# The last two experts of the first mixture-of-experts stage: added to all tokens by one-hot products in place of two indirect stores, and the residual sums loaded earlier

## The chip, the cores and the metric

The kernel runs on one core of one Trainium2 chip. The metric is the device time of one execution in microseconds (us), given as the median of several runs. One execution was profiled; the core's engines are TensorE (PE in the rows, its weight loads PEld), VectorE (DVE), ScalarE (ACT), GpSimd (POOL) and SyncE (SP, which here only starts transfers).

## The reference, cut to what matters

Two decoder layers over 512 tokens of 1024 numbers. Each layer is a mixer and then a hierarchical mixture of 16 experts (of 4 groups one is taken, and of its 4 experts two), both added to the residual x:

```
for layer in range(2):
    h = rms_norm(x, mix_norm)
    x = x + mixer(h)                       # layer 0: state space + gated recurrence; layer 1: sliding-window attention
    h = rms_norm(x, moe_norm[layer])
    # per token: one group, two of its experts, weights "combine"
    hid = silu(h @ w_gate[e]) * (h @ w_up[e]) * combine[:, e]
    x = x + sum over e of hid @ w_down[e]
```

The place of this case is the seam between the first layer's experts and the second layer's attention: `rms_norm(x, ...)` of the second layer needs every expert's contribution to x.

## The kernel before, in words

Tokens stand in four tiles of 128 (TT = 4). A layer's experts (function `experts`, one for each engine) run one after the other, e = 0 to 15. For each one GpSimd fetches up to 128 token rows from a table in memory by an indirect transfer (L479, rows by the list `rows32`), TensorE turns them (`row_turns`, L1906), and multiplies them by gate and up weights (`gate_up`, L1924); ScalarE and VectorE make the gated hidden values; TensorE turns these (`hid_turns`, L1932) and multiplies them by the down weights (`down`, L1948). Every product is made of three f32r products (high and low parts of both operands), so weights and rows are split by ScalarE (high part) and VectorE (low part, by a subtraction).

`down(e)` leaves 128 rows of 1024 results in banks 4 and 5 of PSUM. ScalarE copies them to `yrow[e % 2]` (`result_rows`, L763), and GpSimd adds them to the token rows in memory by an indirect accumulating transfer (`store`, L483). In the first layer that memory is `sums`, into which the residual x was written before the experts began. The store of expert e signals `stored[e % 2]`. GpSimd starts store e once store e - 4 has landed, and ScalarE refills a buffer once its last store has landed.

After the experts each engine passes `experts_over`: it loads a flag into a register (L333) and branches over a body that is only for experts with more than 128 rows (L334). On these inputs the body is not run. Then ScalarE waits for both `stored` semaphores, all 16 stores of the layer (`load_sums`, L800), and loads `sums` into x in four transfers (L802). `norm(2)` on ScalarE takes each tile as it lands: sum of squares (L584), square root (L586), VectorE's reciprocal (L915), the scaled copy `xs` (L596). TensorE turns `xs` (`turn_tile`, L1590), VectorE multiplies by the gain into `hT` (L905), and TensorE makes queries, keys and values (`project`, L2013). `turn_tile(1, 0)` and `project(0, ...)` come first in TensorE's order; the other three tiles are turned behind them.

Weights come through a ring of six slots of 1 MB, refilled by SyncE (L372) as slots are given back. The order on each engine is the order of the code; nothing is reordered.

Of the kernel before, what the change touches and what calls it, by code (L numbers as in the profile page):

```python
# [17 lines left out]
NG, EPG = 4, 4  # L18
# [62 lines left out]
def trunk(nc, x_d, stream_d, cread_d, const_d, param_d, gains_d, out_d):  # L81
# [3 lines left out]
    with ctx:  # L85
        def sb(name, n, dt=f32):
            return ctx.enter_context(nc.sbuf_tensor(name, [P, n], dt))
# [32 lines left out]
            odd.enter_context(nc.sbuf_tensor("odd1", [P, 21504 - 11904 - SLOT], f32))  # L120
            odd_hi = odd.enter_context(nc.sbuf_tensor("odd_hi", [P, SLOT], f32r))[:, :]
        left_hi, left_lo = cut(sb("left_hi", KD * SEQ, f32r), 0, KD, 512), cut(sb("left_lo", KD * SEQ, f32r), 0, KD, 512)
        sb("kept0", 2048)
        w_hi1, w_lo1 = sb("w_hi1", SLOT, f32r), sb("w_lo1", SLOT, f32r)
        sb("kept1", 13312 - 2048 - 2 * SLOT)
        w_hi2, w_lo2 = sb("w_hi2", SLOT, f32r), sb("w_lo2", SLOT, f32r)
# [13 lines left out]
        def out_lo(layer, s):  # L140
            return odd_lo if layer and s == 1 else w_lo[(s + 1 - layer) % 2]

        def expert_pair(layer, m):
            return (2, 1 - layer, layer)[m % 3]

        left_flat = left_hi.rearrange("p k n -> p (k n)")
        row_hi, row_lo = [[cut(left_flat, 1024 * (2 * i + j), KD, 128) for j in range(2)] for i in range(2)]
        low_flat = left_lo.rearrange("p k n -> p (k n)")
        hid_hi, hid_lo = [cut(low_flat, 2560 + 256 * i, 2, 128) for i in range(2)]
        PS = ctx.enter_context(nc.psum_tensor("PS", [P, 8, 512], f32))  # L150

# [90 lines left out]
        w_pair, w_rows, over_weights = sm(2, TT), sm(NE), sm(OVER_TILES)  # L242
        ranks, beyond, flag_f = sm(2 * TT), sm(2 * TT), sm(1)
        group_exp, gap4, gap, gate_sum, pair_sum = sm(TT, 4), sm(TT, 4), sm(TT), sm(TT), sm(TT)
        picked_rank, absent = sm(2 * TT, 16), sm(NE)
        assert at[0] <= 1000, at[0]

        at[0] = S5_END
# [51 lines left out]
        sums_in, weighed, weights_psum = sem("sums_in"), sem("weighed"), sem("weights_psum")  # L300
        rows_made, late_in, first_row_in = sem("rows_made"), sem("late_in"), sem("first_row_in")
        stored = [sem(f"stored{i}") for i in range(2)]

        over = [{n: sem(f"over_{n}{layer}") for n in ("hot", "list_psum", "listed", "weights", "row", "xT_psum", "xT", "gate_up",
                                                      "silu", "hid", "hidT_psum", "hidT", "y_psum", "yrow", "stored")}
# [20 lines left out]
        def used(layer, m):  # L326

            return (NE * EXP_SLOTS + 1) * layer + 1 + m + 1

        def if_over(engine, layer, body):  # L330

# [44 lines left out]
        def _(pool):  # L376
# [109 lines left out]
            def experts(layer):  # L486
                send_rows(layer)
                pool.wait_ge(first_row_in, 16 * (layer + 1))
                pool.wait_ge(rows_in, 16 * (TT - 1) * (layer + 1))
                pool.wait_ge(route_done, layer + 1)  # L490

                def fetch_rows(e):
                    if e >= 2:

                        pool.wait_ge(xT_psum, layer * NE + e - 1)
                    fetch(e % 2, rows32[:, e:e + 1]).then_inc(got_row[e % 2], 16)


                for e in range(4):
                    fetch_rows(e)  # L500
                for e in range(NE):
                    if e + 4 < NE:
                        fetch_rows(e + 4)

                    if e == 0:
                        pool.wait_ge(sums_in, 16 * TT * (layer + 1))
                    if e >= NG:
                        pool.wait_ge(stored[e % 2], 16 * (NE // 2 * layer + (e - NG) // 2 + 1))
                    pool.wait_ge(yrow_done, layer * NE + e + 1)
                    store(layer, e % 2, rows32[:, e:e + 1]).then_inc(stored[e % 2], 16)  # L510

            def experts_over(layer):
                def body(s):
                    for j in range(2):
                        pool.wait_ge(stored[j], 16 * (NE // 2) * (layer + 1))
                    pool.wait_ge(s["listed"], OVER // P)

                    def expert(e, gate_up_at, down_at):

                        pool.dma_start(over_w[:, 0:2 * SLOT].rearrange("p (s n) -> p s n", n=SLOT),  # L520
                                       stream_d[bass.ds(gate_up_at, 2), :, :].rearrange("s p n -> p s n")).then_inc(s["weights"], 16)
                        pool.dma_start(over_w[:, 2 * SLOT:3 * SLOT],
                                       stream_d[bass.ds(down_at, 1), :, :].rearrange("a p n -> (a p) n")).then_inc(s["weights"], 16)
                        for r in range(OVER // P):
                            q = e * (OVER // P) + r
                            nc.gpsimd.tensor_copy(row_now[:, :], over32[:, bass.ds(q, 1)])
                            pool.drain()
# [12 lines left out]
                if_over(pool, layer, body)  # L540
# [2 lines left out]
            experts_over(0)  # L543

            pool.wait_ge(x_in[TT - 1], 48)
            nc.gpsimd.memset(kT1[:, 0:128], 0.0)
            nc.gpsimd.memset(vpad, 0.0).then_inc(at_zero, 1)

# [8 lines left out]
                nc.gpsimd.tensor_tensor(pr, pr, inverse, ALU.mult).then_inc(p_norm, 1)  # L557
            experts(1)
            for j in range(2):
                pool.wait_ge(stored[j], 16 * NE)  # L560
            experts_over(1)


# [1 line left out]
        def _(act):  # L565
# [22 lines left out]
            def norm(occ):  # L588

                for tt in range(TT + 1):  # L590
                    if tt < TT:
                        act.wait_ge(x_in[tt], 48 if occ else 16)
                        deviation(occ, tt, xs[:, tt, :])
                    if tt >= 1:
                        act.wait_ge(rstd_done, TT * occ + tt)
                        act.activation(xs[:, tt - 1, :], x[:, tt - 1, :], ACT.Copy, scale=rstd[:, tt - 1:tt]).then_inc(xs_done, 1)  # L596
# [142 lines left out]
            def experts(layer):  # L739
# [19 lines left out]
                def result_rows(e):  # L759
                    act.wait_ge(w_used, used(layer, down_slot(e)))  # L760
                    if layer or e >= 2:
                        act.wait_ge(stored[e % 2], (base // 2 + e // 2) * 16)
                    act.activation(yrow[e % 2], PS[:, 4:6, :].rearrange("p a b -> p (a b)"), ACT.Copy).then_inc(yrow_done, 1)  # L763

                expert_hi(layer, 2)
                row_his(0, base)
# [1 line left out]
                silu(0)  # L768
                expert_hi(layer, 3)
                for e in range(NE):  # L770
                    if e:
                        result_rows(e - 1)
                    hidden_his(base + e)
                    if e + 1 < NE:
                        expert_hi(layer, down_slot(e))
                    if e + 2 < NE:
                        expert_hi(layer, gate_slot(e + 2))
                        row_his(e % 2, base + e + 2)
                    if e + 2 == NE:
# [17 lines left out]
            def load_sums():  # L797

                for j in range(2):
                    act.wait_ge(stored[j], 16 * (NE // 2))  # L800
                for tt in range(TT):
                    act.dma_start(x[:, tt, :], sums_d[P * tt:P * (tt + 1), :]).then_inc(x_in[tt], 16)  # L802

# [97 lines left out]
        def _(dve):  # L901
# [506 lines left out]
            def experts_over(layer):  # L1408
# [19 lines left out]
                        V.tensor_copy(hidT, PS[:, 3, 0:256].rearrange("p (a b) -> p a b", b=128)).then_inc(s["hidT"], 1)  # L1428
                if_over(dve, layer, body)

            residual(0)
            route(0)
            experts(0)
            experts_over(0)
            for tt in range(TT + 1):
                if tt < TT:
                    inverse(2, tt)
                if tt >= 1:
                    scaled(1, tt - 1)
# [124 lines left out]
        def _(pe):  # L1564
# [333 lines left out]
            def experts(layer):  # L1898
# [36 lines left out]
                def down(e):  # L1935
                    m = down_slot(e)
                    n = base + e
                    pe.wait_ge(hidT_done, n + 1)
                    if layer or e >= 1:
                        pe.wait_ge(yrow_done, n)  # L1940
                    pe.wait_ge(w_lo_done, held(layer, m))
                    pair = expert_pair(layer, m)
                    for half in range(2):
                        for k in range(2):
                            at = k * D + half * 512
                            w = [v[pair][:, at:at + 512] for v in (w_hi, w_lo)]
                            for t, (a, b) in enumerate(((hid_hi[:, k, :], w[0]), (hid_hi[:, k, :], w[1]), (hid_lo[:, k, :], w[0]))):
                                ins = mm(PS[:, 4 + half, :], a, b, start=k == 0 and t == 0, stop=k == 1 and t == 2)  # L1948
                    ins.then_inc(w_used, 1)

                row_turns(0, base, (base // 2 + 1) * 16)
# [45 lines left out]
            experts(0)  # L1997
            experts_over(0)

            turn_tile(1, 0)  # L2000
            def project(tt, part, ks):

# [251 lines left out]
```

## Time and profile before

| | before |
|---|---|
| median of 3 runs | 914.8 us (914.49 to 915.94) |
| the profiled execution | 914.96 us |
| its span, first to last instruction | 913.3 us |
| TensorE busy (matmuls) | 792.9 us, 87% |
| VectorE busy | 584.5 us, 64% |
| ScalarE busy | 476.4 us, 52% |
| GpSimd busy | 172.1 us, 19% |

Busy shares are averages over stages. The first layer's experts run from about 300 to 475 us, attention from about 490 to 670, the second layer's routing and experts after that. Places are given in us from the span's start. A line L763 is line 763 of the kernel before. Small lines are often helpers: L905 is every VectorE operation on two tensors, L908 one with a scalar, L911 one with both, told apart by the tiles they name.

### The profile page before, as it was taken

To read this page: it belongs to the slowest core of one execution; us is meant where nothing else is said; L and a number is where in the kernel's file an instruction comes from. 1 tells how busy PE (TensorE), PEld (TensorE's weight loads), DVE (VectorE), ACT (ScalarE), POOL (GpSimd) and SP (SyncE) were. 2 spreads that over 40 slices of the span, in tenths; PEclk is the share of its full clock that TensorE was granted. 3 is DMA by queue.
4 is the path that set the end of the run, shared out by engine and by line. 5 is a ranking of instruction groups with operands and counts; after the bars stand their busy time and mean duration, and the time that the engine had idled before them with its cause. 6 is when DMAs were issued, how large, how long until landed. Compare 5 with 4: busy or idle time off the path is not lost. (4 is left out here: it accounts for less than half of the span.)

```text
span 913.3 us, 10825 instructions
## 1 busy us (share of the span) xinstructions
PE 792.9 (87%) x4112; PEld 552.4 (60%) x4112; DVE 584.5 (64%) x795; ACT 476.4 (52%) x647; POOL 172.1 (19%) x172
## 2 busy tenths in 40 slices
PE   4999999999897499999972898999899569999983
PEld 3464554554686378877751544545578558887762
DVE  3799756668236488988750356455624649997972
ACT  6051204626224188878744136675733338886872
POOL 4300004100002124333220001030100303332321
PEclk9999999999898599999995999999999679999997
DMA  9222020215425779999983000025043749999962
GB/s 374 98 93 93 2 93 7 86 46 198 195 93 207 287 244 338 329 329 302 328 282 117 1 1 0 1 73 205 1 165 115 312 172 324 338 350 310 318 210 36
DMA packets 31737, 161.50 MB, mean 177 GB/s; under 512 B 7744, under 2 KB 7872, under 8 KB 16320
## 3 DMA queue, kind: packets, MB, share of 16 engines
q1 hardware_dynamic: 17856, 127.93, 37.3%
q0 software_dynamic: 11520, 25.20, 9.9%
q10 hardware_dynamic: 2304, 7.60, 2.2%
q8 instruction: 36, 0.59, 0.3%
q14 instruction: 21, 0.17, 0.1%
HBM read 152.31 MB, written 25.17 MB: 194 GB/s over the span
## 5 line engine op out<-in xcount | busy, mean ns | idle before, releaser
L905 DVE TENSOR_TENSOR w_lo<-ring,w_hi 128x2048 fp32r<-128x2048 f32 x92 | 209.4, 2288 | 53.5 <-ACT w_hi L612 27.8
L1924 PE MATMUL PS<-w_hi,left_hi 128*128 128x512 f32 x512 | 177.1, 408 | 9.2 <-DVE left_hi L905 8.7
L612 ACT ACTIVATE w_hi<-ring 128x2048 fp32r<-128x2048 f32 x86 | 164.1, 1915 | 26.6 <-DMA ring<-stream 25.1
L1924 PEld LDWEIGHTS PS<-w_hi,left_hi 128*128 128x128 f32 x512 | 98.2, 192 | 32.0 <-DVE left_hi L905 12.8
L1924 PE MATMUL PS<-w_lo,left_hi 128*128 128x512 f32 x256 | 101.6, 397 | 0.0
L1948 PE MATMUL PS<-w_hi,left_lo 128*128 128x512 f32 x256 | 85.0, 393 | 5.9 <-DVE left_lo L905 3.3
L2013 PE MATMUL PS<-ring,hT 128*128 128x512 f32 (+1 forms) x192 | 73.6, 536 | 2.7 <-DVE arena L1449 1.9
L479 POOL DMA_INDIRECT arena<-rows x32 | 48.7, 1522 | 82.1 <-PE PS L1906 65.9
L1948 PEld LDWEIGHTS PS<-w_hi,left_lo 128*128 128x128 f32 x256 | 48.1, 188 | 17.9 <-issue 4.2
L1640 PE MATMUL PS<-ring,hT 128*128 128x512 f32 x128 | 57.6, 600 | 0.4 <-ACT arena L668 0.4
L2013 PEld LDWEIGHTS PS<-ring,hT 128*128 128x128 f32 x192 | 36.3, 194 | 35.9 <-issue 33.3
L1640 PE MATMUL PS<-hT,ring 128*128 128x512 f32 x128 | 56.2, 596 | 0.0
L1924 PEld LDWEIGHTS PS<-w_lo,left_hi 128*128 128x128 f32 x256 | 49.2, 192 | 8.3
L905 DVE TENSOR_TENSOR left_hi<-PS,left_hi 128x1024 fp32r<-128x1024 f32 x32 | 39.0, 1219 | 23.4 <-ACT left_hi L748 23.4
L748 ACT ACTIVATE left_hi<-PS 128x1024 fp32r<-128x1024 f32 x32 | 32.4, 1011 | 33.8 <-PE PS L1906 33.8
L1948 PE MATMUL PS<-w_lo,left_lo 128*128 128x512 f32 x128 | 49.9, 390 | 0.0
L668 ACT ACTIVATE arena<-PS 128x512 f32<-128x512 f32 x16 | 9.5, 593 | 76.5 <-PE PS L1640 76.5
L1822 PE MATMUL PS<-w_hi,left_hi 128*128 128x512 f32 x112 | 46.2, 412 | 3.2 <-DVE left_lo L905 2.4
L483 POOL DMA_INDIRECT sums<-hT,rows x16 | 28.3, 1766 | 91.8 <-ACT hT L763 86.7
L483 POOL DMA_INDIRECT out<-hT,rows x16 | 28.2, 1763 | 91.3 <-ACT hT L763 91.3
L1822 PE MATMUL PS<-w_hi,left_lo 128*128 128x512 f32 x112 | 44.7, 399 | 0.0
L763 ACT ACTIVATE hT<-PS 128x1024 f32<-128x1024 f32 x32 | 32.7, 1023 | 22.8 <-PE PS L1948 22.8
(260 smaller groups left out, 1355.0 us busy)
## 6 DMA issues: line engine op xcount, KB each, us to landing
ring<-stream SPq DMA_DIRECT2D x110, 1024.0 KB, 14.1
arena<-stream SPq DMA_DIRECT2D x6, 1024.0 KB
rows<-arena POOLq DMA_DIRECT2D x8, 512.0 KB, 3.1
x<-stream SPq DMA_DIRECT2D x4, 1024.0 KB
x<-x_in SPq DMA_DIRECT2D x4, 512.0 KB, 5.2
x<-x_in ACTq DMA_DIRECT2D x4, 512.0 KB, 6.0
sums<-x POOLq DMA_DIRECT2D x4, 512.0 KB, 4.5
x<-sums ACTq DMA_DIRECT2D x4, 512.0 KB, 5.2
```

The costliest lines, as they stand in the source:

```text
L479: return pool.indirect_dma_start(xrow[j], None, rows_d[:, :], bass.IndirectOffsetOnAxis(index, 0), bounds_check=SEQ - 1, oob_is_err=False)
L483: return pool.indirect_dma_start((sums_d, out_d)[layer][:, :], bass.IndirectOffsetOnAxis(index, 0), yrow[j], None, bounds_check=SEQ - 1, o ...
L612: act.activation(w_hi[pair], held_slot(layer, m), ACT.Copy).then_inc(w_hi_done, 1)
L668: act.activation(dst, PS[:, 7 if i >= 12 else 6 + i % 2, :], ACT.Silu if i // 4 in (1, 3) else ACT.Copy)\
L748: act.activation(row_hi[j], PS[:, 0:2, :].rearrange("p a (b c) -> p (a b) c", c=128), ACT.Copy)\
L763: act.activation(yrow[e % 2], PS[:, 4:6, :].rearrange("p a b -> p (a b)"), ACT.Copy).then_inc(yrow_done, 1)
L905: return V.tensor_tensor(out, a, b, op)
L1640: ins = mm(PS[:, 7 if i >= 12 else 6 + i % 2, :], lhsT[:, m], rhs, start=k == 0, stop=k == KD - 1)
L1822: ins = mm(mixed(layer, s // 2, tt), a, b, start=k == 0 and n == 0, stop=k == KD - 1 and n == 2)
L1924: ins = mm(PS[:, 2, :], a, b, start=k == 0 and t == 0, stop=k == KD - 1 and t == 2)
L1948: ins = mm(PS[:, 4 + half, :], a, b, start=k == 0 and t == 0, stop=k == 1 and t == 2)
L2013: ins = mm(PS[:, 2 + part, 0:n], hT[:, k, tt * 128:tt * 128 + 128], w, start=k == 0, stop=k == KD - 1)
```

## The change

- `experts` on GpSimd no longer stores e = 14 and 15 of the first layer, so each `stored` semaphore counts seven stores there (`stores(1)` = 112).
- ScalarE copies these two experts' results to `last_hi[0]` and `last_hi[1]` (f32r), and VectorE's `split_last` makes their low parts `last_lo` from PSUM. It also builds two one-hot matrices of 128 x 512 from the row lists: a 1 where a row's token is that column's.
- Expert 15's `down` of the first layer goes to banks 6 and 7 and no longer waits for ScalarE's copy of expert 14. In both layers ScalarE takes `hidden_his(15)` before `result_rows(14)`.
- Behind `experts_over(0)` TensorE multiplies, for each token tile, the one-hot matrices by the high and low parts of both experts (`spread`: 32 products of 512 columns). VectorE adds each PSUM tile to x once it is loaded (`add_last`), and the norm waits for that (`summed_in`) in place of the load; for tiles 2 and 3 also for the last product.
- `load_sums` waits for the fourteen stores. GpSimd's two memsets for attention wait for the last product too.

```diff
+        def y_at(layer, e):
+            return 6 if layer == 0 and e == NE - 1 else 4
+        last_hi = [left_flat[:, 2048:3072], low_flat[:, 1024:2048]]
+        last_lo = [left_flat[:, 3072:4096], low_flat[:, 3072:4096]]
+        def stores(layer):
+            return 16 * (NE // 2 - 1) * layer
# GpSimd, experts
+                    if e >= NE - 2 and layer == 0:
+                        continue
                     pool.wait_ge(yrow_done, layer * NE + e + 1)
                     store(layer, e % 2, rows32[:, e:e + 1]).then_inc(stored[e % 2], 16)
# GpSimd, before attention
             pool.wait_ge(x_in[TT - 1], 48)
+            pool.wait_ge(last_psum, TT)
# ScalarE, norm
-                        act.wait_ge(x_in[tt], 48 if occ else 16)
+                        if occ:
+                            act.wait_ge(summed_in, tt + 1)
+                            if tt >= 2:
+                                act.wait_ge(last_psum, TT)
+                        else:
+                            act.wait_ge(x_in[tt], 16)
# ScalarE, experts
                 for e in range(NE):
+                    if e == NE - 1:
+                        hidden_his(base + e)
                     if e:
                         result_rows(e - 1)
-                    hidden_his(base + e)
+                    if e < NE - 1:
+                        hidden_his(base + e)
# ScalarE, load_sums
-                    act.wait_ge(stored[j], 16 * (NE // 2))
+                    act.wait_ge(stored[j], stores(1))
# VectorE
+            def split_last(j):
+                if j == 0:
+                    V.tensor_copy(last_row, rows32[:, NE - 2:NE])
+                    dve.drain()
+                    dve.wait_ge(xT_psum, NE)
+                    for n in range(2):
+                        ts(one_hot[:, n, :], con("time"), last_row[:, n:n + 1], ALU.is_equal)
+                dve.wait_ge(yrow_done, NE - 1 + j)
+                tt_(last_lo[j], PS[:, 4 + 2 * j:6 + 2 * j, :]..., last_hi[j], ALU.subtract).then_inc(last_split, 1)
+            def add_last(tt):
+                dve.wait_ge(x_in[tt], 48)
+                dve.wait_ge(last_psum, tt + 1)
+                at = (4, 0, 2, 6)[tt]
+                tt_(x[:, tt, :], x[:, tt, :], PS[:, at:at + 2, :]..., ALU.add).then_inc(summed_in, 1)
             experts(0)
+            split_last(0)
+            split_last(1)
             experts_over(0)
+            add_last(0)
+            add_last(1)
             for tt in range(TT + 1):
+                if tt + 2 < TT:
+                    add_last(tt + 2)
                 if tt < TT:
                     inverse(2, tt)
# TensorE, down
-                    if layer or e >= 1:
+                    if (layer or e >= 1) and y_at(layer, e) == 4:
                         pe.wait_ge(yrow_done, n)
# TensorE, behind experts_over(0)
+            def spread(j, tt):
+                for half in range(2):
+                    cols = slice(half * 512, half * 512 + 512)
+                    for n, y in enumerate((last_hi[j], last_lo[j])):
+                        ins = mm(PS[:, (4, 0, 2, 6)[tt] + half, :], one_hot[:, j, tt * 128:tt * 128 + 128], y[:, cols],
+                                 start=n == 0 and j == 0, stop=n == 1 and j == 1)
+                return ins
+            pe.wait_ge(last_split, 1)
+            for tt in range(TT - 1):
+                spread(0, tt)
+            pe.wait_ge(last_split, 2)
+            for tt in range(TT):
+                if tt == TT - 1:
+                    spread(0, tt)
+                spread(1, tt).then_inc(last_psum, 1)
             turn_tile(1, 0)
```

## Rows read from the trace of the kernel before

**Rows 1.** Longest waits between 330 and 520 us (who waited <- for whom: total, times, longest).
```profile
PE PS L1590 <- ACT xs L596: 21.1, 2, 20.5
ACT xs L584 <- DMA x<-sums: 14.2, 1, 14.2
```

**Rows 2.** The timeline of all engines around the seam (start us, us, what, idle before).
```profile
462.60 1.96 POOL L483 DMA_INDIRECT sums<-hT,rows  x1 [6.94 <-ACT hT L763]
...
470.42 0.38 ACT L757 ACTIVATE left_lo<-PS 128x256 fp32r<-128x256 f32 x1
470.83 0.42 DVE L905 TENSOR_TENSOR left_lo<-PS,left_lo 128x256 fp32r<-128x256 f32 x1 [2.05 <-ACT left_lo L757]
...
474.38 1.02 ACT L763 ACTIVATE hT<-PS 128x1024 f32<-128x1024 f32 x1 [3.58 <-PE PS L1948]
476.22 1.56 POOL L483 DMA_INDIRECT sums<-hT,rows  x1 [3.32 <-ACT hT L763]
486.19 1.79 ACTq L802 DMA_DIRECT2D x<-sums  x4
489.60 1.06 ACT L584 ACTIVATE xs<-x 128x1024 f32<-128x1024 f32 x1 [14.19 <-DMA x<-sums]
...
493.69 1.13 ACT L596 ACTIVATE xs<-x,small 128x1024 f32<-128x1024 f32 x1
...
494.88 1.97 PE L1590 MATMUL PS<-const,xs 128*128 128x128 f32 x8 [20.54 <-ACT xs L596]
```

**Rows 3.** The same for TensorE alone.
```profile
469.30 0.38 PE L1932 MATMUL PS<-const,hT 128*128 128x128 f32 x2
471.31 0.50 PE L1948 MATMUL PS<-w_hi,left_lo 128*128 128x512 f32 x1 [1.63 <-DVE left_lo L905]
...
497.63 19.02 PE L2013 MATMUL PS<-ring,hT 128*128 128x512 f32 x48 [0.78 <-DVE hT L905]
```

**Rows 4.** The branch at line 334 on each engine: ns min/median/max, first and last start.
```profile
L334 DVEq COMPARE_BRANCH  x2: 63/68/72, 471.7 to 897.9; - x2
L334 PEldq COMPARE_BRANCH  x2: 1760/2773/3786, 472.2 to 898.5; - x2
L334 ACTq COMPARE_BRANCH  x2: 45/48/50, 475.1 to 902.2; - x2
```

**Rows 5.** The four loads of the sums: ns of an issue, then us to landing.
```profile
L802 ACTq DMA_DIRECT2D x<-sums x4: 340/453/455, 486.2 to 487.5; - x4
DMA to landing us min/median/max: 3.4/5.2/7.0
```

**Rows 6.** GpSimd's sixteen accumulating stores of the first layer.
```profile
DMA to landing us min/median/max: 9.0/10.7/11.0
```

**Rows 7.** DMA queues between 474 and 486 us: packets, MB (q0 stores, q1 weights).
```profile
q0 software_dynamic: 230, 0.59, 28.2%
q1 hardware_dynamic: 128, 0.90, 18.3%
```

**Rows 8.** Groups of VectorE's instructions by form, whole span: count, busy us, mean ns.
```profile
L905 DVE TENSOR_TENSOR left_hi<-PS,left_hi 128x1024 fp32r<-128x1024 f32 x32 | 39.0, 1219 | 23.4 <-ACT left_hi L748 23.4
L908 DVE TENSOR_SCALAR arena<-PS,small 128x512 f32<-128x512 f32 x8 | 5.6, 745 | 5.9 <-PE PS L2032 5.9
```

**Rows 9.** Stretches: length, busy PE, PEld, DVE, ACT, POOL; granted clock, DMA share, GB/s.
```profile
305.00:310.00 5.00, 1.70 (x8) 1.57 (x8) 0.00 (x0) 0.00 (x0) 0.00 (x0) 0.50 0.90 320
...
476.00:478.00 2.00, 0.00 (x0) 0.00 (x0) 0.00 (x0) 0.00 (x0) 1.56 (x1) 0.73 0.52 145
500.00:502.00 2.00, 2.00 (x5) 0.84 (x4) 0.00 (x0) 0.00 (x0) 0.00 (x0) 0.79 0.00 0
...
552.00:554.00 2.00, 1.99 (x9) 2.00 (x10) 1.91 (x3) 0.96 (x3) 0.00 (x0) 0.51 0.00 0
554.00:556.00 2.00, 2.00 (x4) 0.73 (x4) 1.85 (x3) 0.59 (x1) 0.00 (x0) 0.64 0.00 0
...
500.00:600.00 100.00, 88.87 (x341) 49.67 (x340) 50.01 (x99) 43.52 (x116) 5.69 (x3) 0.98 0.00 1
```

More of the change, by code:

```diff
@@ L122, in trunk @@
         left_hi, left_lo = cut(sb("left_hi", KD * SEQ, f32r), 0, KD, 512), cut(sb("left_lo", KD * SEQ, f32r), 0, KD, 512)
-        sb("kept0", 2048)
+        one_hot = cut(sb("one_hot", 2048, f32r), 1024, 2, 512)
         w_hi1, w_lo1 = sb("w_hi1", SLOT, f32r), sb("w_lo1", SLOT, f32r)
@@ L244, in trunk @@
         group_exp, gap4, gap, gate_sum, pair_sum = sm(TT, 4), sm(TT, 4), sm(TT), sm(TT), sm(TT)
-        picked_rank, absent = sm(2 * TT, 16), sm(NE)
+        picked_rank, absent, last_row = sm(2 * TT, 16), sm(NE), sm(2)
         assert at[0] <= 1000, at[0]
@@ L302, in trunk @@
         stored = [sem(f"stored{i}") for i in range(2)]
+        last_split, last_psum, summed_in = sem("last_split"), sem("last_psum"), sem("summed_in")
         over = [{n: sem(f"over_{n}{layer}") for n in ("hot", "list_psum", "listed", "weights", "row", "xT_psum", "xT", "gate_up",
@@ L507, in experts @@
                     if e >= NG:
-                        pool.wait_ge(stored[e % 2], 16 * (NE // 2 * layer + (e - NG) // 2 + 1))
+                        pool.wait_ge(stored[e % 2], stores(layer) + 16 * ((e - NG) // 2 + 1))
+                    if e >= NE - 2 and layer == 0:
+                        continue
                     pool.wait_ge(yrow_done, layer * NE + e + 1)
@@ L514, in body @@
                     for j in range(2):
-                        pool.wait_ge(stored[j], 16 * (NE // 2) * (layer + 1))
+                        pool.wait_ge(stored[j], stores(1) + layer * 16 * (NE // 2))
                     pool.wait_ge(s["listed"], OVER // P)
@@ L559, in _ @@
             for j in range(2):
-                pool.wait_ge(stored[j], 16 * NE)
+                pool.wait_ge(stored[j], stores(1) + 16 * (NE // 2))
             experts_over(1)
@@ L761, in result_rows @@
                     if layer or e >= 2:
-                        act.wait_ge(stored[e % 2], (base // 2 + e // 2) * 16)
-                    act.activation(yrow[e % 2], PS[:, 4:6, :].rearrange("p a b -> p (a b)"), ACT.Copy).then_inc(yrow_done, 1)
+                        act.wait_ge(stored[e % 2], stores(layer) + 16 * (e // 2))
+                    kept, at = e >= NE - 2 and layer == 0, y_at(layer, e)
+                    act.activation(last_hi[e % 2] if kept else yrow[e % 2],
+                                   PS[:, at:at + 2, :].rearrange("p a b -> p (a b)"), ACT.Copy).then_inc(yrow_done, 1)
                 expert_hi(layer, 2)
@@ L1429, in experts_over @@
                 if_over(dve, layer, body)
+            def split_last(j):
[6 more added lines that the diff above has]
+                dve.wait_ge(yrow_done, NE - 1 + j)
+                tt_(last_lo[j], PS[:, 4 + 2 * j:6 + 2 * j, :].rearrange("p a b -> p (a b)"), last_hi[j], ALU.subtract).then_inc(last_split, 1)
+            def add_last(tt):
+                dve.wait_ge(x_in[tt], 48)
+                dve.wait_ge(last_psum, tt + 1)
+                at = (4, 0, 2, 6)[tt]
+                tt_(x[:, tt, :], x[:, tt, :], PS[:, at:at + 2, :].rearrange("p a b -> p (a b)"), ALU.add).then_inc(summed_in, 1)
             residual(0)
@@ L1947, in down @@
                             for t, (a, b) in enumerate(((hid_hi[:, k, :], w[0]), (hid_hi[:, k, :], w[1]), (hid_lo[:, k, :], w[0]))):
-                                ins = mm(PS[:, 4 + half, :], a, b, start=k == 0 and t == 0, stop=k == 1 and t == 2)
+                                ins = mm(PS[:, y_at(layer, e) + half, :], a, b, start=k == 0 and t == 0, stop=k == 1 and t == 2)
                     ins.then_inc(w_used, 1)
```

## The prediction

> **What bounds the kernel now.** I read the busy shares by slices first, then the longest waits, then the timeline of the place they name. TensorE is busy 87% of the span and nearly fills most slices; the deepest hole is at about 474 to 495 us. The waits name it: TensorE idles 20.5 us before `turn_tile(1, 0)`, because ScalarE waits 14.2 us for the load of `sums` [rows 1]. In the timeline [rows 2, 3] the reader is to follow one chain: TensorE's last product of expert 15 releases ScalarE's copy at 474.38; GpSimd issues the last store at 476.22; ScalarE issues the four loads at 486.19, so that store took 9.9 us with issue and wake-up, at the foot of the sixteen stores' 9.0 to 11.0 [rows 6]; the first tile lands and the norm starts at 489.60; 5.28 us later TensorE starts, at 494.88, and the first projection at 497.63 [rows 3]. Nothing else is late in this stretch: what moves the loads forward moves all of the second layer.
>
> It does move all of it, because nothing later is tied to absolute time: from 500 to 600 us the DMA engines move nothing [rows 9]. The weight stream waits there for slots that TensorE's own progress frees.
>
> **The change part by part.** Times are of the profiled execution.
>
> *Expert 15's end.* `hid_turns(15)` ends at 469.68 [rows 3]. Before, ScalarE then still copied expert 14's rows and took the hidden high part at 470.42, VectorE its low part at 470.83, and `down(15)` began at 471.31 [rows 2, 3]. Now the high part (0.38) can start at about 469.75, the low part (0.42) at 470.15, and `down(15)` at 470.65, since it has banks 6 and 7 and needn't wait for the copy. That is 0.65 earlier. The twelve products took until 474.38, 3.07 us [rows 2, 3], so the copy of expert 15 (1.02) runs from 473.75 to 474.8. It also needs store 13, issued at 462.60 and landed by 11.0 us later, at 473.6 [rows 2, 6]: close, but before it. The copy of expert 14 goes behind the hidden part and has nothing waiting but `last_lo[0]`.
>
> *Loads.* ScalarE's register load and branch go beside its copy: before, its branch at 475.1 came 0.7 after the copy's start, and took 0.05 [rows 4]. The fourteen stores have landed, so the first load is issued at about 474.55 in place of 486.19. It landed after 3.4 us then [rows 5], with nothing else on the DMA engines. Now 0.90 MB of weights that moved between 474 and 486 [rows 7] are still under way. Four loads (2.1 MB) took 8.3 us from the first issue to the last landing (487.5 + 7.0 - 486.2) [rows 5], so 0.9 MB costs up to 3 us if all of it goes first, and 0 if none. Half, 1.5: tile 0 lands at 479.5 (478.0 to 481.0). The 0.59 MB of stores' packets [rows 7] are gone.
>
> *TensorE's branch.* It was hidden in the 20 us hole and now stands in front of `spread`. TensorE's sequencer reached it at 472.2, about 0.9 us after `down(15)` was let go, and it took 3.79 us, till 476.0; in the second layer 1.76 [rows 4]. The three other engines' took 0.05 to 0.07. From 0.65 earlier: ready at 473.3 (with 1.76) to 475.4 (with 3.79). I take 3.79, since the DMA engines are as busy as before at that point: `spread` starts at 475.4. The Trainium skill (Runtime: NRT & Kernel Launch, Instruction fetch mechanics) says that a taken branch whose target lies outside the fetched pages waits for a DMA fetch of the target page; the trace agrees for TensorE, whose body to be jumped over is the longest, with 3.79 us under DMA load and 1.76 us later on. Were the branch free, `spread` would start at 473.7 and not 475.4, and the sum would be the same, as the load then comes last.
>
> *Spread.* Thirty-two f32r products of 128x512, the same shape as `down`'s, 3.07 / 12 = 0.256 us each: 8.2 us. All of it was nothing before; it lies in the hole. Tile 0 is complete after 16 products, 475.4 + 4.1 = 479.5; the last one at 483.6. VectorE's part: the list copy, two one-hot comparisons (0.75 us each by the nearest row, a multiplication of the same size out of PSUM [rows 8]) between 470.6 and 472.3, `last_lo[0]` (1.22, by the low part of expert rows [rows 8]) to 473.5, `last_lo[1]` from 474.9 to 476.1. Both are there before TensorE asks (475.4, and 478.5 after the first twelve products). If VectorE's one-hot work cost double, 1.5 us more, it would still be covered.
>
> *Adds.* `add_last(0)` waits for the load and the product, both about 479.5, and takes 1.22 [rows 8]: the norm starts at 480.8 in place of 489.60, 8.8 us earlier. `add_last(1)` and `add_last(2)` stand in VectorE's queue ahead of `inverse(2, 0)`, which the norm's copy of tile 0 waits for. The third load lands about two thirds of the way from the first to the last (3.4 to 8.3 after the first issue, so 6.7): 474.55 + 6.7 + 1.5 = 482.8, its add ends at 484.0, the reciprocal at 484.2. The copy of tile 0 began 4.09 us after the norm's start [rows 2], so it asks at 484.9. Covered by 0.7; if the third load comes 2 us later, 1.3 us of the gain go. TensorE turns tile 0 at 486.1 and projects at 488.8. GpSimd's memsets and the other tiles' adds (the last ends near 486) have until the 48 products of tile 0 end, 19 us later [rows 3].
>
> *Clock.* TensorE's granted clock fell at about 476.9, 2.5 us after its last product, and came back at about 500.8 (0.73 and 0.79 in those two stretches [rows 9]), so 3.2 us of the projection and the turning ran at 1.2 GHz instead of 2.4, which cost 1.6 and some 0.7 us. After the change TensorE idles only from 483.6 to 486.1. At 552 it fell too, after a short pause, and was back after 3.4 us of dense work (0.51 and 0.64 [rows 9]). Such a stretch would cover the turning and the first microsecond of the projection and cost 1.3. I take a gain of 1.0, bounds 0 and 2.3.
>
> *Second layer's end.* The new order on ScalarE also holds there, but `down(15)` still waits for expert 14's copy. Something between 0 and 0.65; I take 0.2.
>
> Sum: 8.8 + 1.0 + 0.2 = 10.0. The profiled execution took 914.96 us (span 913.3 and 1.7 around it), the median is 914.8: 904.96, or 904.8 on the median's scale. Bounds: the best is load and product with nothing in the way (478.0, gain 10.3) with all of the clock's 2.3 and 0.65, -13.2; the poorest is tile 0 landing at 481.0 and the third load late, 8.8 - 1.5 - 1.3 = 6.0. Later short low-clock stretches can come or go, each worth 3.4 / 2 = 1.7 us.
>
> **The rivals.**
>
> *More: the clock stays at 2.4 GHz and the loads aren't hindered.* For it: TensorE's pause is 2.5 us, just as long as the clock took to fall. Against: it fell after other pauses of that size. 901.6 to 903.
>
> *Less: loads or fetch come late.* The four loads share with the rest of the weights, tile 0 lands at 481 or later, or the third load holds up `inverse(2, 0)`. For it: DMA share 0.52 at 476 [rows 9] with stores and weights together. Against: the stores' part vanishes. 907 to 909.
>
> *No change.* Something else releases the loads at the old time, such as a store of the fourteen that lands late, or the second layer waits on what moves in absolute time. Nothing in the rows speaks for it: store 13 was issued at 462.60. 914.8.
>
> *Slower: the low clock lasts through the projection.* From 305 to 310 the clock was at half while TensorE did a little work now and then [rows 9]. If the scattered end of `spread` and the turning bring about such a stretch, and it goes on while tile 0 is projected, its 48 products (19.02 - 1.6 = 17.4 at full clock) take 17.4 us more, against gains of 8.8 + 0.2 and the 2.3 lost before: +6.1, 920.9. It decides from 2 x 11.3 = 22.6 us of low clock under dense work. Against it: under dense work the clock came back within 6 us at 495 and 3.4 us at 552.
>
> **How the numbers follow.** The forecast, 904.8 with 902.8 to 907 as its own spread, 0.66. More, 0.12; less, 0.14; no change, 0.04; slower, 0.04. What a measurement of this kernel can tell from no change is about 0.2%, 1.8 us. Faster by over that: 0.66 + 0.12 + 0.14 = 0.92. For 8 in 10 the range takes in the forecast and most of more and less: 901.8 to 908.4.
>
> **What would show it.** In the changed kernel: ScalarE's load issues at about 474.5 and no store behind 462.6; TensorE's branch again of 2 to 4 us and the one-hot products from about 475.4, 32 of them in 7 to 8 us; the norm's first square sum at about 480.8, released by VectorE's add; the turning at 486.1 and the projection at 488.8; a low clock of some 3 us there in place of 24. The prediction is wrong if the first add waits for anything but load or product, if the norm of tile 0 waits for `add_last(2)` by more than 1 us, if TensorE's start behind 486 is not followed by the same attention and expert stages as before, shifted as a whole, or if the time lies above 909.

## The result, and the profile after

| | before | changed |
|---|---|---|
| median of the first comparison, 6 runs each | 914.45 us (912.67 to 915.94) | 909.29 us (907.16 to 910.21) |
| ratio, 95% interval | | 0.9937 (0.992 to 0.9954) |
| the profiled execution | 914.96 us | 910.21 us |

The change makes the kernel 5.2 us faster by the medians, 0.56%, where 10 was forecast and 908.4 was the range's upper end. In two further comparisons the same kernel came out at 0.9918 (0.9899 to 0.9936) and 0.9943 (0.9929 to 0.9957), so by the three ratios it gains 5.2 to 7.5 us. Single executions of one kernel spread over 3 us and more, which matters below. Two executions in a slow state, one of `again_three` (974 us) and one of the kernel before (1401 us), at granted clocks of 0.82 and 0.56, are left out of the medians.

The page of the changed kernel: TensorE has 9.6 us more to do in a span 4.8 us shorter. The last line gives the median time to landing of the four loads of the sums.

```profile
span 908.5 us, 10901 instructions
PE 802.5 (88%) x4144; PEld 559.1 (62%) x4144; DVE 592.3 (65%) x804; ACT 476.0 (52%) x647; POOL 168.7 (19%) x170
...
x<-sums ACTq DMA_DIRECT2D x4, 512.0 KB, 7.8
```

The seam in the changed kernel's timeline, to be laid beside [rows 2, 3] (line numbers have moved: L826 issues the loads, L2052 is `spread`, L598 the norm's square sum, L1637 the turning, L2077 the projection; `left_hi` and `left_lo` name the memory that `last_hi` and `last_lo` share):

```profile
476.12 2.54 ACTq L826 DMA_DIRECT2D x<-sums  x4
...
477.63 3.04 PE L2052 MATMUL PS<-left_hi,one_hot 128*128 128x512 f32 x12 [2.52 <-DVE left_lo L929]
480.50 2.88 PE L2052 MATMUL PS<-left_lo,one_hot 128*128 128x512 f32 x12
482.35 1.22 DVE L929 TENSOR_TENSOR x<-x,PS 128x1024 f32<-128x1024 f32 x1 [4.93 <-DMA x<-sums]
...
483.61 1.06 ACT L598 ACTIVATE xs<-x 128x1024 f32<-128x1024 f32 x1 [7.44 <-DVE x L929]
...
488.90 1.10 PE L1637 MATMUL PS<-const,xs 128*128 128x128 f32 x8 [3.70 <-ACT xs L615]
...
490.94 2.07 PE L2077 MATMUL PS<-ring,hT 128*128 128x512 f32 x2 [0.93 <-DVE hT L929]
```

The reader is to see three things. The loads go out as forecast, 5.4 us after expert 15's hidden turning (forecast: 5.25; the turning itself came at 470.77, 1.5 us later than before). `spread` begins at 477.6, 0.8 us later than forecast once that shift is taken off. And VectorE's add, the step that releases the norm, is put down to the load, at 482.35 where 479.5 was forecast: 1.5 us of this is the shift, 1.4 us are its own. The first tile's products were complete at 481.57, so the load was last by only 0.8 us.

TensorE's branch, of both layers, as in [rows 4]:

```profile
L345 PEldq COMPARE_BRANCH  x2: 3483/4012/4542, 473.0 to 894.0; - x2
```

The granted clock behind the seam (eighth number), as in [rows 9]:

```profile
490.00:492.00 2.00, 1.07 (x3) 0.55 (x3) 0.95 (x3) 2.00 (x3) 0.00 (x0) 0.50 0.04 8
...
496.00:498.00 2.00, 2.00 (x5) 0.91 (x4) 0.00 (x0) 0.00 (x0) 0.00 (x0) 0.83 0.00 0
...
518.00:520.00 2.00, 2.00 (x3) 0.67 (x2) 1.55 (x3) 0.31 (x1) 0.00 (x0) 0.50 0.00 0
```

The clock is at 1.2 GHz from 489.8 to 496.7, while the projection runs, and again from 517.2 to 520.6, where the kernel before had none.

### The profile page after: what moved, and what is told of

It is laid out like the page before. It is cut to its first block and busy times, and to the rows that moved or that the text cites. A ratio compares the mean times of both kernels' runs of the same rounds, so it can differ in the third digit from the quotient of the medians.

```text
span 908.5 us, 10901 instructions
## 1 busy us (share of the span) xinstructions
PE 802.5 (88%) x4144; PEld 559.1 (62%) x4144; DVE 592.3 (65%) x804; ACT 476.0 (52%) x647; POOL 168.7 (19%) x170
## 5 line engine op out<-in xcount | busy, mean ns | idle before, releaser
L1971 PE MATMUL PS<-w_lo,left_hi 128*128 128x512 f32 x256 | 102.1, 399 | 0.0
L2077 PE MATMUL PS<-ring,hT 128*128 128x512 f32 (+1 forms) x192 | 76.4, 552 | 2.9 <-DVE arena L1496 1.9
L2077 PEld LDWEIGHTS PS<-ring,hT 128*128 128x128 f32 x192 | 37.3, 199 | 37.7 <-issue 35.1
L1869 PE MATMUL PS<-w_lo,left_hi 128*128 128x512 f32 x112 | 44.4, 396 | 0.0
L571 POOL TENSOR_TENSOR arena<-arena,small 128x1024 f32<-128x1024 f32 x8 | 15.2, 1899 | 153.0 <-DVE small L1555 153.0
```

The source lines that it names most:

```text
L1869: ins = mm(mixed(layer, s // 2, tt), a, b, start=k == 0 and n == 0, stop=k == KD - 1 and n == 2)
L1971: ins = mm(PS[:, 2, :], a, b, start=k == 0 and t == 0, stop=k == KD - 1 and t == 2)
L2077: ins = mm(PS[:, 2 + part, 0:n], hT[:, k, tt * 128:tt * 128 + 128], w, start=k == 0, stop=k == KD - 1)
```

## The experiments

The runs came in three groups, each on one chip with its own runs of the kernel before. Medians are compared within a group, or through the ratio to before. Landmarks of the profiled executions, in us from the span's start:

| kernel | expert 15's hidden turning | norm's start | first turning | first projection | second turning | last projection |
|---|---|---|---|---|---|---|
| before | 469.3 | 489.6 | 494.9 | 497.6 | 516.5 | 623.7 |
| changed | 470.8 | 483.6 | 488.9 | 490.9 | 511.1 | 619.7 |
| `again` | 468.9 | 483.3 | 488.6 | 490.6 | 511.0 | 619.8 |
| `again_three` | 468.4 | 482.6 | 487.9 | 489.9 | 508.9 | 616.1 |
| `no_products` | 467.9 | 481.9 | 487.2 | 489.9 | 510.1 | 618.8 |
| `branch_behind` | 470.5 | 483.9 | 489.2 | 491.9 | 511.5 | 620.7 |
| `fill_gap` | 469.9 | 484.0 | 493.5 | 495.5 | 512.8 | 621.3 |
| `fill_four` | 468.6 | 483.2 | 488.4 | 490.5 | 507.8 | 616.4 |
| `weights_held` | 468.4 | 479.5 | 484.7 | 486.8 | 505.5 | 612.6 |
| `held_again` | 468.5 | 480.4 | 485.7 | 487.8 | 507.8 | 616.4 |
| `held_four` | 469.1 | 480.4 | 485.7 | 487.7 | 508.1 | 616.9 |
| `weights_held_branch_behind` | 469.9 | 479.9 | 485.2 | 487.9 | 506.7 | 613.9 |
| `held_fill_three` | 469.5 | 482.5 | 487.8 | 489.8 | 507.1 | 616.4 |
| `before_filled` | 470.2 | 490.8 | 496.1 | 498.1 | 515.4 | 624.3 |

**`again`: the changed kernel, a second profile.**

> The changed kernel once more, for a second profile and its spread. Clock theory: the seam gains about 8 us up to the first projection in every execution, and the rest of the gap to the forecast 10 lies in stretches at 1.2 GHz that come and go between executions of the same kernel (3.4 us each, 1.7 us of work lost); so this profile shows expert 15's hidden turning and the attention at other distances from those of the first profile, by steps of 1.7, and the median lies 5 to 6 us below before. Rival, a cost that the change brings to the experts ahead of the seam: expert 15's hidden turning is again 1.5 us later than before (470.8 against 469.3).

Median 906.76 us, ratio 0.9918 (0.9899 to 0.9936): 7.5 us below before by the ratio, more than the 5 to 6 expected. The hidden turning came at 468.9, 1.9 us earlier than in the first profile, so the 1.5 us lost ahead of the seam are no cost of the change; in the first profile TensorE ran at 1.2 GHz from 452.3 to 455.7, here it did not. But the norm started only 0.3 us earlier. Neither theory had said that. What set the norm's start did not move with the experts:

```profile
474.32 2.38 ACTq L826 DMA_DIRECT2D x<-sums  x4
475.99 4.61 PE L2052 MATMUL PS<-left_hi,one_hot 128*128 128x512 f32 x12 [2.75 <-DVE left_lo L929]
480.43 2.91 PE L2052 MATMUL PS<-left_lo,one_hot 128*128 128x512 f32 x12
482.06 3.55 DVE L929 TENSOR_TENSOR x<-x,PS 128x1024 f32<-128x1024 f32 x3 [6.47 <-DMA x<-sums]
```

```profile
DMA to landing us min/median/max: 7.7/8.8/9.6
```

Loads issued at 474.3 landed from 482.0 on: 7.7 us for the first where [rows 5] had 3.4. Here the clock was low for the first products (476.3 to 479.7), and even so the load came last, though by only 0.5 us: the first tile's products were complete at 481.52. The last weight load had been issued 1.9 us earlier than in the first profile (468.1 against 470.0), but it landed no earlier, after 13.7 us against 11.6, at 481.9 against 481.6. The landing of the sums' first tile is close to it in both, 482.0 and 482.3.

**`no_products`: the waiting alone, without the two experts' share.** The edit is shown against the changed kernel and cut; experts 14 and 15 are missing from this kernel's sum.

```diff
             experts(0)
-            split_last(0)
-            split_last(1)
             experts_over(0)
-            add_last(0)
-            add_last(1)
...
-            pe.wait_ge(last_split, 1)
-            for tt in range(TT - 1):
-                spread(0, tt)
...
-                            act.wait_ge(summed_in, tt + 1)
+                        act.wait_ge(x_in[tt], 48 if occ else 16)
```

> Only the waiting is changed: no stores of experts 14 and 15 in the first layer, loads behind fourteen stores, new order on ScalarE and expert 15 in banks 6 and 7, but no low parts, no one-hot products, no adds; the two experts' share is left out of the sum. It shows what the products and adds cost in the seam. By the seam's times the norm starts with the landing of tile 0 at 481.5 rather than at 483.5: 2.0 us faster than the changed kernel up to there. Clock theory: TensorE pauses from 475 to 487, the clock falls as before and the projection's start pays 2.3 us, so the whole is about equal to the changed kernel, 0 to 2 us faster. Rival, the products are the dear part: over 3 us faster than the changed kernel.

Median 908.5, 1.7 slower than the changed kernel of its group (906.76); 0 to 2 faster was expected. The two ratios, 0.9927 (0.9909 to 0.9945) and 0.9918 (0.9899 to 0.9936), overlap, so only the rival, over 3 us faster, is ruled out clearly. The loads went out at 474.01 and the norm started with the landing at 481.90, 7.9 us later. With no products at all the load lands as late as in `again`, and the norm starts only 1.4 us earlier, by the add that is left out: products and adds were not the dear part. The clock was low from 475.3 to 495.8, as with a hole, and takes most of that back: the projection starts 0.7 us earlier, the second turning 0.8.

**`branch_behind`: TensorE's branch behind the products.**

```diff
             experts(0)
-            experts_over(0)
             def spread(j, tt): ...
             ...
+            experts_over(0)
             turn_tile(1, 0)
```

> TensorE's flag branch put behind the one-hot products in place of ahead of them (the body of the branch isn't run on these inputs). Theory that the branch is late on the path: the products start at about 475.1 instead of 477.6, tile 0 of them is ready by 479.7, and the norm then starts with the load of tile 0 (landed at 481.5): 0.7 us earlier, and no more, since the load is next; the branch takes its 2 to 4.5 us under the norm. Time 0.7 us below the changed kernel, but the pause of TensorE ahead of the turning gets 2.5 us longer, which may cost up to 1.7 us of clock. Rival, that branch and products are what holds the seam back (the whole 1.2 us that it came later than forecast): 1.2 to 2.5 us below.

The products started at 474.68, straight behind the expert's own, and VectorE's wait for tile 0 of them ended at 478.5. In the first profile that was 481.6, still 0.8 us ahead of the load. It did nothing for the norm's start, and the 0.7 us expected did not come: the add still waited 5.47 us for the load, which landed at 482.6, 4.1 us behind the products. The pause ahead of the turning grew to 7.0 us, the clock was low from 486.4 to 496.6, and the kernel is 3.1 us slower than the changed one (909.83 against 906.76).

```profile
482.63 1.22 DVE L929 TENSOR_TENSOR x<-x,PS 128x1024 f32<-128x1024 f32 x1 [5.47 <-DMA x<-sums]
...
489.17 1.97 PE L1637 MATMUL PS<-const,xs 128*128 128x128 f32 x8 [7.02 <-ACT xs L615]
```

**`fill_gap` and `fill_four`: useless products in TensorE's pause.**

```diff
                 spread(1, tt).then_inc(last_psum, 1)
+            pe.wait_ge(summed_in, 1)
+            for _ in range(9):       # fill_four: 4
+                mm(PS[:, 5, :], ident, con("time"), start=True, stop=True)
             turn_tile(1, 0)
```

> Nine products of 128x512 in f32 of no use are added on TensorE behind the one-hot products (into a bank already read), about 3.9 us at 2.4 GHz, so that it is busy until the second layer's first turning. Clock theory: the 6.8 us at 1.2 GHz from 489.8 on vanish, tile 0's projection takes 17.4 instead of 20.1 us, and the kernel is 2.5 to 3.4 us faster than the changed one. Rival, that the clock falls there whatever TensorE does or that the projection's length isn't on the path: within 0.5 us of the changed kernel.

> As the run with nine useless products, with four: nine took 7.9 us and held the turning back to 493.5 (the f32 form takes 0.88 us a piece, not the 0.43 that I had put down). Four take 3.5 us, until 488.8, when the turning is due. Clock theory: no stretch at 1.2 GHz from 489.8, tile 0's projection and what follows up to the second turning takes 17.3 us (as with nine) and not 20.1, so 2.5 to 3 us faster than the changed kernel. Rival, the clock falls there anyway: same time as the changed kernel.

Nine took 7.9 us and put the turning off to 493.5: 911.63 us, a failed experiment on time. Still, from the first turning to the second it took 19.3 us, against 22.2 and 22.4 in the changed kernel's first two profiles and 21.6 before; low clock in the projection cost those two 2.9 and 3.1 us. Four are the right size (the same 19.3 us), with 0.20 us left of the pause:

```profile
484.64 3.59 PE L2066 MATMUL PS<-const 128*128 128x512 f32 x8
488.43 1.09 PE L1637 MATMUL PS<-const,xs 128*128 128x128 f32 x8 [0.20 <-ACT xs L615]
```

Its ratio, 0.9917 (0.9891 to 0.9942), is that of the changed kernel's best comparison (0.9918). On one chip it wasn't set beside it, so a gain of 1 to 2 us isn't excluded; the 2.5 to 3 expected did not show.

**`before_filled`: the hole of the kernel before filled with 20 such products.**

> The kernel before with 20 useless f32 products of 128x512 (17.5 us) on TensorE in its hole, from 476.1 to 493.6, into a free bank. It prices the low clock in the kernel before by itself: the stretch from 477 to 501 at 1.2 GHz vanishes, and the turning and projection of tile 0 gain 2.3 us: 2.3 us faster than before. Rival, that the hole costs nothing in clock: same as before.

The expectation failed in the time and held in the place: ratio 1.000 (0.9986 to 1.0014), though the first turning to the second took 19.3 us in place of 21.6. Most of what was gained came back in a stretch at 1.2 GHz behind the second turning, from 521.9 to 525.3 (about 1.7 us of 2.3), that the kernel before did not have:

```profile
522.00:524.00 2.00, 2.00 (x3) 0.67 (x2) 1.62 (x4) 0.31 (x1) 0.00 (x0) 0.50 0.00 0
524.00:526.00 2.00, 2.00 (x5) 0.88 (x4) 1.61 (x3) 0.00 (x0) 0.00 (x0) 0.67 0.00 0
```

This profile is of the slowest of the kernel's twelve executions (917.56 us): it was 1.2 us late at the norm's start and lost 1.9 us more behind the last projection, so it shows where the clock moved but does not add up to the equal medians.

**`weights_held`, `held_again`, `held_four`: weight loads held back until the sums have landed.**

```diff
+                if i == QKV0 + 3:        # held_four: QKV0 + 2
+                    sp.wait_ge(x_in[TT - 1], 48)
                 sp.dma_start(slot(i), stream_d[i, :, :]).then_inc(slot_full[r % RING], 16)
```

> The changed kernel with three weight loads of the second layer (slots QKV0+3, QKV0+4 and OUT1, 1 MB each, issued at 464 to 470 and needed at 500 and later) held back until the fourth load of the sums has landed. Theory that the sums' loads stand behind weights on the DMA engines: tile 0 lands 3.4 to 4.2 us after its issue in place of 5.4 to 7.9, at about 479 to 480, and what comes last is then the one-hot products' first tile (481.5 to 482): the norm starts at 483, 0.5 us earlier than in the changed kernel, no more. Rival, that the loads themselves are slow for another reason (four at once behind an accumulating store): landing stays at 5.4 us or more.

904.47 us, ratio 0.9887 (0.9861 to 0.9914): 9.5 us below before by the medians, 10.3 by the ratio. The first load landed after 4.3 us, and the norm started at 479.5, 3.9 us earlier than in `again`. I had expected 0.5, with the products next at 481.5; but TensorE's branch took 3.45 us here and not 4.8, and the clock was high in `spread`, so tile 0 was ready at 478.1, together with the load. The 3.9 us are therefore not the landing's alone: with the products where `again` had them the edit would have won some 0.5.

```profile
473.77 2.52 ACTq L828 DMA_DIRECT2D x<-sums  x4
474.17 3.02 PE L2054 MATMUL PS<-left_hi,one_hot 128*128 128x512 f32 x12 [1.41 <-issue]
...
478.19 2.35 DVE L931 TENSOR_TENSOR x<-x,PS 128x1024 f32<-128x1024 f32 x2 [3.12 <-PE PS L2054]
479.45 1.06 ACT L600 ACTIVATE xs<-x 128x1024 f32<-128x1024 f32 x1 [5.64 <-DVE x L931]
```

```profile
DMA to landing us min/median/max: 4.3/5.6/6.8
```

DMA queues from 474 to 482 us, of `again` and then of this kernel, where the weights moved nothing (q10 carries the sums, q1 the weights):

```profile
q10 hardware_dynamic: 481, 1.77, 63.1%
q1 hardware_dynamic: 115, 0.80, 24.0%
```

```profile
q10 hardware_dynamic: 576, 2.10, 75.2%
```

The repeat and the version with four, with the changed kernel in their group:

> The changed kernel a third time, on the chip of the next three runs, as their measure. Theory (the loads of the sums stand behind 1 MB weight loads): wherever expert 15's turning falls, between 468.9 and 470.8, tile 0 lands at about 482 and the projection starts at 490.6 to 491. Median 905.5 to 909.5.

> The run with three weight loads held back once more, beside the changed kernel on one chip, since its profiled execution (901.85) lay 2.6 below its median. Theory: norm's start 11.0 us after expert 15's turning again (14.4 in the changed kernel's second profile), tile 0 landed after 3.4 to 4.3 us; 3 to 5 us faster than the changed kernel. Rival, a lucky place of the low-clock stretches: norm's start as early, but a gain of under 2 us.

> Four weight loads held back (from slot QKV0+2 on). With three, tile 0 lands at 478.1 and its product is ready at about 478.9 behind TensorE's branch. Theory: the landing has nothing more to give, the product is last, so norm's start and time stay within 1 us of the run with three; the fourth held load lands in time for its use 7 us into the projection. Rival, weights in flight are still what delays: up to 1 us earlier; or the projection now waits for its weights: 1 to 3 us slower.

`again_three` had a median of 909.0 us (906.07 to 910.75) and a first landing after 7.6, `held_again` had 904.52 (902.22 to 906.91; ratio 0.9883, 0.9863 to 0.9902): 4.5 us less on one chip by the medians, 5.5 by the ratios. Each has only five executions and their ranges touch, but the two ratios' intervals are apart. `held_four` had 905.08 (0.9892, 0.9876 to 0.9907), no better; the fourth load in flight cost nothing in time. In `held_again` the first load took 5.3 us and was last, and the norm started 11.9 us after the hidden turning, not 11.0; in `held_four` the load took 3.3 us, the products were last, and it was 11.3.

**`weights_held_branch_behind`: both edits.**

> Both: the three weight loads held back, and TensorE's flag branch behind the one-hot products. Theory that loads and branch each hide the other: the products' tile 0 is ready at about 479, the load lands at about 479 to 480, the norm starts at 480.5 to 481.5 (that is the forecast's 480.8), 2 to 3 us earlier than in the changed kernel, and the projection at about 489; TensorE's pause and the low clock remain, so the time is 1.5 to 3 us below the changed kernel's. If either alone had been the bound, this kernel would be no better than the one with that edit alone.

The norm started 10.0 us after the hidden turning against 11.0 and 11.9 with the weights alone held, with tile 0 of the products ready at 478.0 and the load landed at 478.6, after 3.3 us: the branch's edit alone had left the load in the way (13.4 us), and the weights' edit alone the branch or the rest of the load, by 1 to 2 us. The median, 904.61 (0.9899, 0.9874 to 0.9923), is that of `weights_held` (904.47, same chip): TensorE's pause grew from 3.0 to 3.6 us, its turning ran at 1.2 GHz, and the clock was low for 6.8 us where the profile of `weights_held` had 3.4. The low clock need not come from the edit, since `held_again` and `held_four` had 6.8 us too. The edit also presumes that the branch's body isn't run.

**`held_fill_three`: weights held and the pause filled.**

> Three weight loads held back, and three useless f32 products (2.6 us) in TensorE's pause of 3.0 us ahead of the turning. Theory of the clock: the 3.4 us at 1.2 GHz in the projection's start vanish, 1.4 to 1.7 us shorter from the turning to the second turning (20.75 to 19.2), but a stretch of 3.4 us may come in the sparse place behind it (between the second turning and the next projection), as in the kernel before when filled, which takes it back: 0 to 1.7 us faster than the run with three held. Rival, a filled pause keeps the clock up everywhere: 1.5 us faster or more.

904.43 us (0.9886, 0.9871 to 0.9901), equal to `held_again`. First to second turning 19.3 us against 22.1, but in this profile the low clock had moved ahead, into the one-hot products (476.9 to 480.3), which put the norm's start off to 482.5: the load landed at 478.1, after 3.2 us, and the products' first tile was ready only at 481.1. With the weights held but the products at 1.2 GHz the norm starts 13.0 us after the hidden turning. Here too the filler had no net gain.

## Why the prediction was wrong

The mechanism was right: the seam was the place, the loads went out 10.1 to 12.5 us earlier, and the second layer followed as a whole. Two terms of the sum were mis-sized, and a third cost, low clock in `spread`, was not in it.

*Loads.* This is the step that failed. It put tile 0's landing 4.95 us after the issue, 3.4 and half of the 3 us that 0.90 MB of weights would cost. Measured: 6.2 us in the first profile, 7.7 and 7.6 in the two others, 7.9 without any products, and 3.2 to 5.3 with the weights held. The load was the last to arrive in all three profiles of the changed kernel, by 0.8, 0.5 and 0.2 us: right behind it stood the one-hot products, so a load on time would have won no more than that. From the hidden turning to the norm's start the forecast had 11.5 us; it was 12.8, 14.4 and 14.2, and 11.0 to 11.9 with the weights held and the products at full clock. The upper bound for the weights, 3 us, was too low as well: up to 4.5 came, and the prediction's own rate, 8.3 us for 2.1 MB, gives 3.6 for 0.90 MB. The bytes were right (0.80 MB moved beside the sums in `again`), the price was not. What the runs show in its place is that tile 0 lands with the last of the weights, not halfway: in the six profiles that have both landings, the first tile's came from 0.9 us before to 0.8 us behind the last weight load's (in the changed kernel 482.3, 482.0 and 481.3 against 481.6, 481.9 and 481.8). Why is open in part. A weight packet is 0.80 MB / 115 = 7.0 KB on average, and one of the sums 1.77 MB / 481 = 3.7 KB. If an engine takes packets of both in turn, the sums get about a third of it while it has weights left. The Trainium skill (DMA: Bandwidth & Descriptors, Queues, rings and completion order) says that each engine goes round its queues packet by packet; no row here shows the turn on one engine. Over all 16 engines together the share was not a third. From 476 to 480 us of `again`:

```profile
q10 hardware_dynamic: 272, 1.02, 74.5%
q1 hardware_dynamic: 52, 0.37, 21.8%
```

By 480 the sums had moved 1.1 MB, twice the 0.52 MB of tile 0, which still landed only at 482.0. That fits a rest of the weights on a few of the engines, with the load complete only when its part on the last of them is; the packets' rows don't name the engine, so this is argued and not shown. In the kernel before, the wait for the last stores had given these weights the time to pass unseen.

*Expert 15's end.* Its 0.65 us were right: `down(15)` began 1.31 us after the hidden turning in place of 2.01. They did not reach the norm's start, since the landing didn't follow.

*TensorE's branch.* Forecast 3.79, measured 4.5 to 4.9 in six profiles with weights under way, 3.5 to 3.8 in the four with weights held. Traffic alone does not decide it: the kernel before took 3.79 and, filled, 3.89 beside the same weights, and in the second layer, where the prediction read 1.76 as the branch under less load, `before_filled` took 3.91 with the DMA engines 26% busy (898 to 906 us), the kernel before 1.76 at 29% (896 to 903). That it stood in front of `spread` was right; branch and products were covered by the late load in the changed kernel. With weights held the products were last in `held_four` by 1.4 us, level with the load in `weights_held`, and first by 0.9 in `held_again`.

*Spread, split and adds.* Thirty-two products took 7.6 us in the first profile (forecast 8.2), but 9.2 in the two others, where the clock was at 1.2 GHz from 476.3 to 479.7; the prediction had no term for that. Counted from the hidden turning, the first tile's products were complete after 10.8, 12.6 and 12.7 us, where 10.2 was forecast. A comparison took 0.48 (0.75), an add 1.22. `inverse(2, 0)` did not wait for `add_last(2)` by more than 0.05 us. The rest of this term was as forecast.

*Clock.* This is the second mis-sized term. Forecast: a gain of 1.0 with 0 as the lower bound. From the first turning to the second it took 22.2, 22.4 and 21.0 us, against 21.6 before: on average nothing gained. In two of the three profiles a further 3.4 us stretch came at 517, which cost 1.7; in the third, none. From the first projection to the last, the changed kernel took 128.8, 129.1 and 126.2 us, the kernel before 126.1. So between -0.1 and -3.0 there. The forecast's +1.0 also held the turning, which did gain 0.7 us: counted from the first turning to the last projection it is -2.0, -2.3 and +0.6 where +1.0 stood. Which of these stretches falls where differs between executions of one kernel, and one profile of before cannot say which is usual; that before itself stood on the good side there is possible and not shown.

*Second layer's end.* From expert 15's hidden turning there to TensorE's last product it took 4.8 us in place of 5.1; 0.2 was forecast.

Added up for the first profile: norm and first turning came 2.8 us later than forecast (483.6 for 480.8), 1.5 of it brought along from ahead of the seam and 1.3 by the landing. The turning at full clock won 0.7, so the first projection was 6.7 us earlier than before for 8.8 forecast. Then 2.7 were lost up to the last projection, and 0.8 won behind it: 4.8 in the span. The rival called "less" named the mechanism and the place, tile 0's landing at 481 or later, with 907 to 909 us; it held 0.14 and came closest, with medians of 906.8 to 909.3 in the three comparisons.

With held weights the kernel came out 9.5 and 10.2 us below before by the medians, for a forecast of 10, and the norm started 11.0 and 11.9 us after the hidden turning, for 11.5. That the seam could give what was forecast is shown; that the whole sum fits is in part luck, since the two profiles' spans are 13.2 and 8.0 us below before's, and behind the norm's start they won 3.0 and lost 1.1 us against it.

## What to carry to other kernels

When a wait is removed that let a queue drain, count what is still in flight at the new time, and expect the moved transfer to land when the last of that does, not after its share of the bytes. Look at what stands right behind it as well: here the products came only 0.2 to 0.8 us ahead of the load, so a repair of the load alone would have won no more. A transfer that is on the path can be protected by holding back the ones that aren't due: one added wait on the weight queue was worth about 4.5 us, nearly as much as the change itself, though part of that came with faster products and a shorter branch. A gain of granted clock goes into a sum with both signs: here filled pauses moved the low stretch elsewhere.

## What the runs showed of the hardware

A compare-and-branch of TensorE's sequencer took 3.5 to 4.9 us ahead of the one-hot products but 0.36 and 0.37 us when the same branch over the same body stood behind them (`branch_behind`, and with the weights held). In the second layer of these two kernels it took 3.76 and 3.90, and 1.76 to 3.91 over all profiles:

```profile
L345 PEldq COMPARE_BRANCH  x2: 363/2062/3760, 478.8 to 893.4; - x2
```

So it isn't the length of the body alone. Where the code lies, or how long the sequencer had stood at a wait before it, may decide; neither was separated. A product of 128x512 with plain f32 operands shows as two rows and took 0.88 us at 2.4 GHz (nine in 7.9 us), where one of f32r takes 0.23.
